# Neighbourhood attention with query tiles of 16 grid columns and keys of 32, in a float32 encoder layer

## What is computed

```python
col_start = np.clip(c - NA_WIN_COLS // 2, 0, GRID_W - NA_WIN_COLS).reshape(NA_NCB, NA_QCB)
kblk_start = np.clip(np.arange(NA_NCB) * NA_QCB - NA_WIN_COLS // 2, 0, GRID_W - NA_KCB)
...
logits = jnp.einsum('bjqhd,bwjkhd->bhjqwk', qb, k_blk).astype(jnp.float32)
bias = jnp.transpose(table[:, dr_idx][:, :, dc_idx], (0, 2, 3, 1, 4))
logits = jnp.where(mask, logits + bias, -jnp.inf)
p = jax.nn.softmax(logits, axis=(-2, -1)).astype(v.dtype)
out = jnp.einsum('bhjqwk,bwjkhd->bjqhd', p, v_blk)
```

## Time and profile before

| | us |
|---|---|
| median of 3 runs | 2284.01 |
| lowest and highest run | 2282.57, 2286.64 |
| the profiled execution | 2284.7 |
| its span | 2282.8 |

### The profile page before, as it was taken

The page is one execution under the profiler, slowest core; times in us unless marked ns, Lnnn a source line. Parts: engine busy times, 40 slices in busy tenths (PEclk is TensorE's granted clock), DMA queues, the critical chain, the costliest instruction groups (busy, mean ns, idle before and its releaser), DMA issues.

```text
span 2282.8 us, 30905 instructions
## 1 busy us (share of the span) xinstructions
PE 2187.5 (96%) x12116; PEld 1897.2 (83%) x12116; DVE 1602.6 (70%) x1267; ACT 1392.4 (61%) x1115; POOL 161.4 (7%) x116
## 2 busy tenths in 40 slices
PE   6999999999992999999999999999999999999997
PEld 5867878888781999988999889998889988899886
DVE  5366354223417788888888888888888888888885
ACT  5365345222312677777777777777776777767774
POOL 2102200000010000100101001010010100101010
PEclk9999999999995999999999999999999999999999
DMA  5111110112423799999999999999999999999995
GB/s 224 62 48 35 56 62 25 56 56 90 180 86 115 283 366 376 373 368 380 364 375 371 364 375 367 375 374 367 378 361 378 370 371 377 358 382 366 374 371 186
DMA packets 68927, 618.75 MB, mean 271 GB/s; under 512 B 8112, under 2 KB 8496, under 8 KB 16144
## 3 DMA queue, kind: packets, MB, share of 16 engines
q1 hardware_dynamic: 61632, 592.47, 67.1%
q0 software_dynamic: 6816, 25.30, 3.9%
q10 hardware_dynamic: 432, 0.34, 0.0%
HBM read 605.50 MB, written 12.58 MB: 271 GB/s over the span
## 4 chain that ended last, share of the span: by engine, by line
PE 86%; DVE 5%; ACT 4%; issue 3%; DMA 1%; POOL 0%; ACTq 0%; DVEq 0%; POOLq 0%
PE PS L412 26%; PE PS L414 26%; PE PS L413 26%; PE PS L488 2%; DVE x_w_low L947 2%; PE PS L500 2%; ACT x_w_high L875 2%; PE PS L694 1%; PE PS L512 1%; PE PS L421 1%; DVE hidden L1250 1%; PE PS L600 1%; DMA gathered<-t_dram,idxi 0%; ACT s L785 0%; ACT w_high L713 0%
## 5 line engine op out<-in xcount | busy, mean ns | idle before, releaser
L947 DVE TENSOR_TENSOR x_w_low<-x_w_raw,x_w_high 128x2816 fp32r<-128x2816 f32 (+2 forms) x384 | 1182.6, 3090 | 246.7 <-ACT x_w_high L875 245.4
L875 ACT ACTIVATE x_w_high<-x_w_raw 128x2816 fp32r<-128x2816 f32 (+2 forms) x384 | 978.8, 2557 | 249.0 <-PE PS L414 213.8
L412 PE MATMUL PS<-x_w_high,xT_high 128*96 128x352 f32 x2048 | 667.1, 326 | 1.4 <-DVE xT_low L947 1.4
L414 PE MATMUL PS<-x_w_high,xT_low 128*96 128x352 f32 x2048 | 660.2, 322 | 0.0
L413 PE MATMUL PS<-x_w_low,xT_high 128*96 128x352 f32 x2048 | 657.5, 321 | 0.0
L412 PEld LDWEIGHTS PS<-x_w_high,xT_high 128*96 128x96 f32 x2048 | 330.1, 161 | 6.6 <-issue 4.3
L413 PEld LDWEIGHTS PS<-x_w_low,xT_high 128*96 128x96 f32 x2048 | 332.3, 162 | 2.4
L414 PEld LDWEIGHTS PS<-x_w_high,xT_low 128*96 128x96 f32 x2048 | 331.5, 162 | 1.5
L412 PE MATMUL PS<-x_w_high,hidden_high 128*96 128x512 f32 x704 | 280.0, 398 | 2.3
L413 PE MATMUL PS<-x_w_low,hidden_high 128*96 128x512 f32 x704 | 278.1, 395 | 0.0
L414 PE MATMUL PS<-x_w_high,hidden_low 128*96 128x512 f32 x704 | 277.8, 395 | 0.0
(11 more groups left out here) (146 smaller groups left out, 1819.0 us busy)
## 6 DMA issues: line engine op xcount, KB each, us to landing
x_w_raw<-in_w_expert_gate SPq DMA_DIRECT2D x128, 1408.0 KB, 8.2
x_w_raw<-in_w_expert_up SPq DMA_DIRECT2D x128, 1408.0 KB, 8.6
x_w_raw<-in_w_expert_down SPq DMA_DIRECT2D x96, 1536.0 KB, 8.2
x_w_raw<-in_w_expert_down SPq DMA_DIRECT2D x32, 1024.0 KB, 6.8
w_raw<-in_w_in SPq DMA_DIRECT2D x20, 1024.0 KB, 4.8
x<-in_x_sample SPq DMA_DIRECT2D x8, 512.0 KB, 14.2
w_raw<-in_w_out SPq DMA_DIRECT2D x4, 1024.0 KB, 5.0
bias<-in_bias_na POOLq DMA_DIRECT2D x8, 448.0 KB, 3.5
```

Source lines behind the costliest of these rows:

```text
L412: mm(out, sh, mh, start=first, stop=False)
L414: return mm(out, sl, mh, start=False, stop=last)
L875: a_(xh[:, w % SPLITS, 0:n], xraw[:, w % RAWS, 0:n], ACT.Copy).then_inc(x_high, 1)
L947: return v.tensor_tensor(out, src, high.bitcast(F32), ALU.subtract)
```

## The change

The sample's 512 tokens are cut into four query tiles by columns: tile j holds the columns 16j to 16j+15 of all 8 grid rows (128 queries), and its keys are the 32 columns from `WINDOWS[j]` (0, 8, 24, 32) of all 8 rows (256 keys). So every item of neighbourhood attention has 256 keys. The prompt's items stay as they were.

- Queries: ACT writes a sample query tile of `qT` in two pieces, one for each grid row, into tile order. Keys stay in token order; PE reads them in eight runs of 32 tokens.
- Values: the products need 128 consecutive keys on 128 partitions, so SP stores the four sample tiles of `v` into a DRAM buffer (256 KB each), waits for them, and loads eight blocks back (two for each window, each four grid rows of 32 columns, 256 KB). PE waits for all eight before the first sample value product. Two of the windows lie where the sample's `v` tiles were.
- Bias: two tables in place of one, 128 x 384 a head for the prompt (of which an item reads 256 columns), 128 x 1024 for the sample.
- Order: all prompt items of all heads come first (16), then all sample items (32). There are 16 bias loads where there were 8.
- Output: the sample's token tiles are in tile order, and the merge stage's evacuations put them back in token order.

The core of the diff:

```diff
+        vw = [at(f"v_windows{i}", off, 2048).rearrange("p (w h n) -> p w h n", w=2, h=2)
+              for i, off in enumerate((38848, 42944))]
...
+        s_na = at("s_na", 40896, 4 * NW).rearrange("p (b m n) -> p b m n", b=4, m=1)
+        bias_w = at("bias_windows", 44992, 8 * NW).rearrange("p (b n) -> p b n", b=2)
+        aT_na = at("aT_na", 47808, 2 * NW).rearrange("p (b n) -> p b n", b=2)
...
-        def items(heads):
-            return [(h, qt, t0, nt) for h in range(heads) for (t0, nt) in GROUPS for qt in range(nt)]
-
-        ATT = {"diff": items(4), "na": items(8)}
-        HPI = NT
+        ATT = {"diff": [(h, qt, t0, nt) for h in range(4) for (t0, nt) in GROUPS for qt in range(nt)],
+               "na": [(h, qt, t0, 2) for (t0, nt) in GROUPS for h in range(8) for qt in range(nt)]}
...
+        BIAS = [("diff", h, NT, bias_diff[h], bias[:, h % 2, :]) for h in range(4)]
+        BIAS += [("na", h, 2, bias_prompt[h], bias_w[:, h % 2, 0:PW]) for h in range(8)]
+        BIAS += [("na", h, 4, bias_sample[h], bias_w[:, h % 2, :]) for h in range(8)]
...
+                if kind == "gate_d0":
+
+                    for t in range(2, NT):
+                        sp.wait_ge(S("pn", "pused"), 2 * NT + t + 1)
+                        sp.dma_start(v_dram[(t - 2) * P:(t - 1) * P, :], vv[:, t, :]).then_inc(s_vst, 16)
+                    sp.wait_ge(s_vst, 64)
+                    grid = v_dram.rearrange("(r c) n -> r c n", c=GW)
+                    for j, c0 in enumerate(WINDOWS):
+                        for half in range(2):
+                            sp.dma_start(vw[j // 2][:, j % 2, half, :], grid[4 * half:4 * half + 4, c0:c0 + 32, :]
+                                         ).then_inc(s_vw, 16)
...
-                    br, used = ("diff", nh - 1) if nh - 2 < 4 else ("na", nh - 5)
-                    pool.wait_ge(S(br, "biased"), HPI * used)
-                pool.dma_start(bias[:, b, :], bias_diff[nh] if nh < 4 else bias_na[nh - 4]).then_inc(s_b[b], 16)
+                    pool.wait_ge(S(BIAS[nh - 2][0], "biased"), bias_first(nh - 2) + BIAS[nh - 2][2])
+                pool.dma_start(BIAS[nh][4], BIAS[nh][3]).then_inc(s_b[b], 16)
...
+                            if br == "na" and t0 == 2:
+                                keys = kT[r][:, c, SP_:N].rearrange("p (r c) -> p r c", c=GW)[
+                                    :, :, WINDOWS[qt]:WINDOWS[qt] + 32]
+                            i = mm(PS[:, nm * (step % ring) + m, 0:nt * P], queries, keys, start=True, stop=True)
...
+                        if windowed and h == 0 and qt == 0:
+                            pe.wait_ge(s_vw, 16 * 8)
...
+                            values = vw[qt // 2][:, qt % 2, c, :] if windowed else vv[:, t0 + c, :]
+                            i = mm(PS[:, 6 + a % 2, 0:w], turned[:, a % 2, c * P:(c + 1) * P],
+                                   values[:, h * w:(h + 1) * w], start=c == 0, stop=c == nt - 1)
...
+                    for row in range(2):
+                        r = 2 * (t - 2) + row
+                        into = qT[:, :, SP_:N].rearrange("p c (j r q) -> p c r j q", j=4, r=8)[:, :, r]
+                        i = a_(into, src.rearrange("p c (r j q) -> p c r j q", r=2, j=4)[:, :, row], ACT.Copy,
+                               scale=gain)
...
+                            dst = yTh[:, :, cols] if t < 2 else window_order(yTh[:, :, SP_:N])[:, :, t - 2]
+                            high_t("g", NT + t, dst, S("g", "yn_t"), t + 1)
```

More of the change, by code:

```diff
@@ L42 @@
 BW = 896
-NA_ROWS = 15
+PW = 384
+NW = 256
+GW = 64
+WINDOWS = [0, 8, 24, 32]
 GROUPS = [(0, 2), (2, 4)]
@@ L357, in _ @@
             norm_rs("pn", 12, 8)
-            for nh in range(6, 12):
+            for nh in range(6, len(BIAS)):
                 load_bias(nh)
@@ L745, in evac_t @@
                 gain = gains[:, g0 + c:g0 + c + 1]
-                if c == 0:
+                if c == 0 and stage == "pn" and t >= 2:
+                    for row in range(2):
[3 more added lines that the diff above has]
+                               scale=gain)
+                elif c == 0:
                     i = a_(qT[:, :, t * P:(t + 1) * P], src, ACT.Copy, scale=gain)
@@ L776, in attend @@
                 nm = 2 if br == "diff" else 1
+                maps, turned = (sT, aT) if br == "diff" else (s_na, aT_na)
                 for step in range(len(L) + 3):
@@ L799, in attend @@
                             act.wait_ge(S(br, "pv"), a - 1)
-                        a_(aT[:, a % 2, 0:n], PS[:, 4 + a % 2, 0:n], ACT.Copy).then_inc(S(br, "aT"), 1)
+                        a_(turned[:, a % 2, 0:n], PS[:, 4 + a % 2, 0:n], ACT.Copy).then_inc(S(br, "aT"), 1)
                 act.wait_ge(S(br, "aT"), len(L))
@@ L1038, in attend @@
                 nm = 2 if br == "diff" else 1
+                maps = sT if br == "diff" else s_na
                 for step in range(len(L) + 5):
@@ L1050, in attend @@
                             dve.wait_ge(S(br, "tr"), a - 3)
-                        c0 = 384 - 128 * qt
+                        c0 = {"diff": 384 - 128 * qt, "na": 128 - 128 * qt if t0 == 0 else NW * qt}[br]
                         for m in range(nm):
                             i = v.tensor_tensor_reduce(
-                                out=sT[:, a % 4, m, 0:n], in0=PS[:, nm * (a % (4 // nm)) + m, 0:n], in1=bias[:, b, c0:c0 + n],
+                                out=maps[:, a % 4, m, 0:n], in0=PS[:, nm * (a % (4 // nm)) + m, 0:n],
+                                in1=BIAS[nh][4][:, c0:c0 + n],
                                 scale=-1.0, scalar=3.0e38, op0=ALU.add, op1=ALU.min,
@@ L1124, in _ @@
                     elif kind == "gate_n0":
-                        low_t("g", NT + t, yTl[:, :, cols], yTh[:, :, cols])
+                        dl, dh = ((a[:, :, cols] if t < 2 else window_order(a[:, :, SP_:N])[:, :, t - 2])
+                                  for a in (yTl, yTh))
+                        low_t("g", NT + t, dl, dh)
                     elif kind == "gate_n1":
@@ L1303, in _diff_bias, with _prompt_bias, _sample_bias @@
     return np.ascontiguousarray(rel_bias[bucket[at]].transpose(2, 0, 1))
-def _na_bias(rpb):
+def _prompt_bias(rpb):
     import numpy as np
-    out = np.full((8, P, 14, 64), -1e30, np.float32)
-    col = np.arange(64)
-    start = np.clip(col - 8, 0, 48)
-    for c in range(64):
+    out = np.full((8, P, PW // GW, GW), -1e30, np.float32)
+    start = np.clip(np.arange(GW) - 8, 0, 48)
+    for c in range(GW):
         kc = np.arange(start[c], start[c] + 16)
         for rr in range(2):
-            out[:, 64 * rr + c, :, kc] = rpb[:, 1 - rr:15 - rr, kc - c + 15].transpose(2, 0, 1)
-    return out.reshape(8, P, BW)
+            out[:, GW * rr + c, :, kc] = rpb[:, 5 - rr:11 - rr, kc - c + 15].transpose(2, 0, 1)
+    return out.reshape(8, P, PW)
+def _sample_bias(rpb):
+    import numpy as np
+    out = np.full((8, 8, 16, 4, 8, 32), -1e30, np.float32)
+    for c in range(GW):
+        start = min(max(c - 8, 0), 48)
+        kc = np.arange(start, start + 16)
+        for r in range(8):
+            out[:, r, c % 16, c // 16, :, kc - WINDOWS[c // 16]] = rpb[:, 7 - r:15 - r, kc - c + 15].transpose(2, 0, 1)
+    return out.reshape(8, P, 4 * NW)
 def kernel(**inputs):
@@ L1346 @@
     give("bias_diff", _diff_bias(np.asarray(inputs["rel_bias"])))
-    give("bias_na", _na_bias(one["na_rpb"]))
+    give("bias_prompt", _prompt_bias(one["na_rpb"]))
+    give("bias_sample", _sample_bias(one["na_rpb"]))
     for name in ("w_branch_diff", "w_branch_na", "w_out"):
```

35 lines of the change are left out of this document (22 added, 13 removed).

## The result

The changed kernel takes 2269.68 us (median of four runs, 2268.81 to 2270.82) and the kernel before, in the same comparison, 2285.07 (2282.57 to 2286.64): a ratio of 0.9934, 95% interval 0.9917 to 0.9951. It is faster by 15.4 us. I had forecast 32, and 2252.0 us; the time lies outside my range of 2248 to 2260. The direction was right and the size was half.

A forecast was written before the change was run, and what follows sets the result against it. PE, busy 96% of the span, was taken to bound the kernel: -34.0 us of work and +2.1 us of bias waits make -31.9 from 2284.7, 2252.8; with the median 0.7 lower, 2252 us, range 2248 to 2260.

The forecast's parts named there:

- What the change does to PE: Neighbourhood attention: 32 sample items fall from 2.14 to 1.05 us each on PE, taking off 34.0 us after a hidden part.
- The bias loads: Prompt part of attention: four bias loads in a chain, each waiting for a buffer's release, make PE wait 2.1 us.
- L: Time for one bias load in the chain of four to land, taken as 3.1 us.
- Values via HBM: Attention: value windows stored and reloaded are there at 313 us, PE needs them at 325 to 327: price 0.
- SP's next unit load: On SP during attention: it queues behind the value windows, but its unit is needed only after attention: price 0.
- The clock: PE's first wait in attention, 3.9 us, drops the granted clock, but a later bias wait absorbs it: 0, at most 1.5 us.
- The few rings: Rival, 25%: four of 16 rings carry the window loads, which take 20 us; bias loads lose 3.7 us: 2253.5 us.
- The crowded bias loads: Rival, 10%: the first prompt bias lands after 9.6 us and the clock's 1.5 us are not hidden: 2260 us.
- The low clock through the prompt part: Rival, 3%: all 16 prompt items run at twice 1.05 us, 17 us more: 2269 us.
- Strided keys: Rival, 3%: PE reads the sample's keys, eight runs of 32, at half speed, 14 us more: 2266 us.
- PE waits over 6 us in the prompt part: A sign, in attention's prompt part, that the forecast is wrong; the forecast expected PE to wait 2 to 4 us there.

The follow-up runs named there:

- without windows: The changed kernel without storing or loading values via HBM, the sample's value products taking two fixed value tiles: 2259.8 us (one run).
- prompt bias ahead: The changed kernel with all eight prompt bias tables in buffers of their own, loaded before attention: 2265.14 us, 0.9927 of the kernel before.
- windows on all rings: The changed kernel with sample keys and bias column by column, so window loads have outermost count 16 in place of 4: 2260.34 us, 0.9907 of the kernel before.
- rings and bias ahead: The changed kernel with column-major window loads over 16 rings and prompt bias tables loaded before attention: 2253.01 us, 0.9862 of the kernel before.
- late split: The kernel before, with only the second gate unit's split moved behind the last attention item: 2281.46 us, 0.9984 of the kernel before.

## Why the prediction was right or wrong, point by point

The work taken from PE was right; two other terms of the sum failed. PE's waits for the bias loads were forecast at 2.1 us and measured at 7.8, because I priced the window traffic beside them at 0. The clock was forecast at 0 and took 9.8: it fell in the first wait and again with the waits for bias.

- **What the change does to PE**, 34.0 us: right. A sample item takes 1.05 us, and with the clock held the stretch has 48.7 to 49.0 us of work where 48.8 were forecast. ACT and DVE follow at that pace: the timeline above has no gap on PE at the stretch's end.
- **The bias loads**, 2.1 us: the chain of four is there as I wrote it, but the term was mis-sized. It was sized with L = 3.1, a lone load and a little more; without windows L is 2.7 and PE waits 1.3 us, but with them each link took 6.0 to 8.5 us and PE waits 7.8. I named the sharing ("the value windows share the rings at first") and gave it 0.2 us a landing.
- **Values via HBM**, there at 313 with "12 us of slack, price 0": wrong, and the root of the step before. Where PE was early enough to wait for them (prompt bias ahead) they were there at 335; on all rings each landed within 8.0 us of its issue. Without them, and with the unit loads back in their old place, the stretch is 10.5 us shorter; the windows on all rings give 8.3. PE pays this not by waiting for values but by the bias loads, which got slower beside this traffic, and by the clock behind those waits. I also had SP's next unit load at 0 because nothing waits for it; that it crosses the bias loads I did not see.
- **The clock**, "the drop comes out of that wait: 0, and 1.5 as the other end": wrong, and the largest error, 9.8 us. I had one drop in mind, and the recovery of the earlier trace rows, eight passes of 512 columns in one go, as its price. Here there were three drops, and after the first one PE worked at 0.50 from 307.5 to 319.7, with one wait of 2.25 us in it. I set the cost of a wait and the cost of the clock side by side, where a wait for bias can buy more time at the low clock.
- **The rivals.** The few rings were there as described: the Trainium skill's count (DMA: Bandwidth & Descriptors, Why a DMA increments its semaphore by 16 and not by 1) gives four, and the rows of 312 to 314 us agree with a DMA share of 0.26 at 99 GB/s, against 104 worked out. I gave this rival the right mechanism, a chance of one in four and a price of 1.6 us, since I let L grow to 3.5 only. The crowded bias loads, one in ten and 2260 us, came close too, but made one landing slow and gave the clock 1.5 us; here every link of the chain was slow. The low clock through the prompt part, 3%, came to 2269, the time measured, and that is coincidence: it had 17 us of clock and no further waits, and the runs show 9.8 and 5.7. Its "against", that solid work brings the clock back, held: with the rings and the bias loads ahead it took 5.4 us of work, 309.3 to 314.7. But in the changed kernel waits broke that work up. The Trainium skill's rule beside it (TensorE: Matmul & The Clock Gate, HAM oscillation), that pieces of work each followed by a wait for DMA start at the low clock, is borne out here in part: the pieces after the waits of 3.92, 2.25 and 3.71 us began at 0.50; the one after 1.67 us began at 1.00 and fell to 0.50 some 1.3 us later, and with the windows on all rings the one after 1.38 us stayed at 1.00. Strided keys cost nothing: the pitch is 0.44 us either way.
- **What would show it.** The mark "PE waits over 6 us in the prompt part" was set well: it is the one that tripped. The merge stage kept its length.
- **Two slips in the sums** change nothing: at half the rate a lone prompt bias comes to 3.5 - 1.2 = 2.3 us and not 2.4, and -30.3 from 2284.0 is 2253.7 and not 2253.5.

## What to carry to other kernels

When work on the bound engine halves, every load whose buffer is freed by that work has half the time, so size such a chain with the rings as they will then be filled, and give a load that others must not wait for a layout that spreads over all rings. Count a long wait of TensorE twice where the granted clock falls in it, once for itself and once for the clock after it, and take waits away together. Against the kernel before, measured beside each, the change alone takes off 15.4 us, with the rings 22.5, with the early loads 17.7, and with both 31.8, about the 32 forecast. Look also for work like the late split that stands ahead of a stage and is needed only behind it: moving it gave 3.4 us in the old kernel and 4.7 on top of the other two.

## What the runs showed of the hardware that I had not expected

- The length of the last wait alone does not tell whether the clock drops: 3.07 us before the first transposes left it at 1.00 in the kernel before, and in the changed one it fell some 1.3 us after the end of a wait of 1.67 us at 325.3, where PE had waited twice before (3.92 and 2.25 us).
- From the end of the wait of 3.92 us, the clock needed 5.4 us of short matmuls without a break to come back in one kernel (309.3 to 314.7, rings and bias ahead), and 12.2 us with one wait of 0.65 us in it (309.7 to 321.9, no windows). Behind the wait of 3.35 us it came back 2.9 us into the eight passes of 512 columns (128.74 to 131.6):

```profile
131.00:132.00 1.00, 1.00 (x3) 0.30 (x2) 0.00 (x0) 0.19 (x1) 0.00 (x0) 0.68 1.00 418
```

- Loads on four rings delay others: a 1 MB unit load behind the windows landed after 19.4 us, and after 10.2 with the windows on all rings; without windows another unit's load landed after 4.9.
- Issuing itself took long on SP: 15.6 us for the eight windows on four rings, as shown here for the changed kernel with the unit loads behind them, and 5.1 us for the eight on all rings. That full rings held SP is likely, but no view shows it.

```profile
304.68 15.61 SPq L338 DMA_DIRECT2D v_windows<-v_dram  x8
320.33 3.65 SPq L317 DMA_DIRECT2D w_raw<-in_w_branch_diff  x1
324.01 0.52 SPq L317 DMA_DIRECT2D w_raw<-in_w_in  x1
```

- With all rings busy the windows moved at 255 GB/s and not at 418. Why is open; no run took it apart.
